# Summing gathered expert rows on TensorE in column strips, with up and down gathers alternating in sets of four

## The reference, cut to what matters

```python
u_sel = jnp.take(expert_down, ib, axis=0)
act = jnp.einsum('tkd,td->tk', u_sel.astype(jnp.float32), hb.astype(jnp.float32))
w = gb * jax.nn.gelu(act, approximate=False)
v_sel = jnp.take(expert_up, ib, axis=0)
return jnp.einsum('tk,tkd->td', w, v_sel.astype(jnp.float32))
```

## Time and profile before

| | |
|---|---|
| three timed runs | 4560.25, 4561.05, 4565.51 us (median 4561.05) |
| span of the profiled execution | 4559.0 us, 21846 instructions; no separate time of this execution is given |
| DVE busy | 3389.3 us, 74% |
| POOL busy | 2108.9 us, 46% |
| PE busy | 1629.2 us, 36% |
| queue of POOL's gathers | 147456 packets, 1073.81 MB, 57.7% of 16 engines' span |

### The profile page before, as it was taken

How to read it: one execution, slowest core, us unless ns; L and a number is a source line. 1 busy time by engine, 2 the same in 40 slices (tenths; PEclk the granted TensorE clock), 3 DMA queues, 4 the chain that set the end, 5 groups by cost and what they waited for, 6 DMA issues and landing times. The chain is left out here.

```text
span 4559.0 us, 21846 instructions
## 1 busy us (share of the span) xinstructions
PE 1629.2 (36%) x5521; PEld 961.5 (21%) x5521; DVE 3389.3 (74%) x4309; ACT 397.1 (9%) x780; POOL 2108.9 (46%) x1162
## 2 busy tenths in 40 slices
PE   8999978998900000000000099888000000000000
PEld 6444434444800000000000066457000000000000
DVE  3777795301099999999999913411999999999999
ACT  1111114300100000000000013301000000000000
POOL 0000000000076777776777700000777767767767
PEclk9999989999955555555555599799555555555555
DMA  6343422344399999999999953132999999999999
GB/s 201 111 110 112 117 67 85 103 142 144 126 411 397 379 398 400 378 396 394 388 394 400 374 159 132 56 129 76 405 387 394 400 382 394 408 384 390 398 389 377
DMA packets 283029, 1286.59 MB, mean 282 GB/s; under 512 B 46993, under 2 KB 56033, under 8 KB 150881
## 3 DMA queue, kind: packets, MB, share of 16 engines
q0 software_dynamic: 147456, 1073.81, 57.7%
q1 hardware_dynamic: 100400, 200.81, 13.6%
q10 hardware_dynamic: 35120, 11.33, 1.0%
HBM read 1283.77 MB, written 2.10 MB: 282 GB/s over the span
## 5 line engine op out<-in xcount | busy, mean ns | idle before, releaser
L1578 DVE SCALAR_TENSOR_TENSOR xs<-big,sc,xs 128x2048 f32<-128x2048 f32 x512 | 1203.7, 2351 | 51.0 <-DVE sc L1568 2.1
L1560 DVE CUSTOM_DVE_ANT_0 big<-big,hs 128x2048 f32<-128x2048 f32 x512 | 1137.8, 2286 | 34.8 <-remote 10.3
L488 POOL DMA_INDIRECT big<-in_peer_down,sc x256 | 518.2, 2024 | 638.0 <-issue 635.4
L531 PE MATMUL bank<-wring,ht 128*128 128x512 f32 (+1 forms) x1792 | 778.5, 592 | 3.3 <-ACT ht L888 1.7
L488 POOL DMA_INDIRECT big<-in_peer_u,sc x256 | 518.2, 2024 | 405.0 <-DVE sc L1547 320.4
L488 POOL DMA_INDIRECT big<-in_peer_up,sc x256 | 506.0, 1977 | 247.6 <-DVE xs L1578 172.2
L488 POOL DMA_INDIRECT big<-in_peer_v,sc x256 | 506.1, 1977 | 246.6 <-DVE xs L1578 171.1
L772 PE MATMUL bank<-cn,sc 80*128 80x80 f32 x1 | 0.4, 393 | 1381.4 <-DMA sc<-in_rec_out_norm_g 1381.4
L531 PEld LDWEIGHTS bank<-wring,ht 128*128 128x128 f32 x1792 | 339.7, 192 | 402.1 <-issue 395.9
L545 PE MATMUL bank<-ht,wring 128*128 128x256 f32 x1792 | 387.9, 379 | 2.6 <-ACT ht L888 2.6
L545 PEld LDWEIGHTS bank<-ht,wring 128*128 128x128 f32 x1792 | 340.2, 190 | 49.6 <-issue 2.4
(11 more groups left out here) (308 smaller groups left out, 2055.2 us busy)
## 6 DMA issues: line engine op xcount, KB each, us to landing
wring<-in_w_in SPq DMA_DIRECT2D x84, 1024.0 KB, 5.3
wring<-in_w_out SPq DMA_DIRECT2D x32, 1024.0 KB, 5.0
wring<-in_w_attn_o SPq DMA_DIRECT2D x16, 1024.0 KB, 5.1
wring<-in_peer_w_query SPq DMA_DIRECT2D x16, 1024.0 KB, 5.0
wring<-in_peer_w_q SPq DMA_DIRECT2D x16, 1024.0 KB, 5.0
wring<-in_glu_w_a SPq DMA_DIRECT2D x8, 1024.0 KB, 5.0
wring<-in_glu_w_b SPq DMA_DIRECT2D x8, 1024.0 KB, 5.0
big<-in_peer_down,sc POOLq DMA_INDIRECT x256, 9.5
```

The source lines that it names most:

```text
L488: pool.indirect_dma_start(out=gslot[:, slot, :], out_offset=None, in_=table[0], in_offset=bass.IndirectOffsetOnAxis(ap=usub(rST)[:, b * TO ...
L531: mm = pe.matmul(dense_bank[2 * pair + t][:, 0:w_cols], lhs[:, k, t * P:(t + 1) * P], wslot[:, b, kk * w_cols:(kk + 1) * w_cols], start=(k ...
L1560: v.tensor_tensor_reduce(gslot[:, slot, :], gslot[:, slot, :], h[:, t, :], 1.0, 0.0, ALU.mult, ALU.add, sub(rAC)[:, b * TOPK + kk:b * TOPK ...
L1578: v.scalar_tensor_tensor(x[:, t, :], gslot[:, slot, :], wt[:, kk:kk + 1], x[:, t, :], ALU.mult, ALU.add).then_inc(gused[slot], 1)
```

## The change

The dots stay on DVE as they are. The sum over the up rows moves to TensorE:

- An up gather still brings 128 rows of 8 KB, but now 16 experts of 8 tokens: partition 16 i + k holds expert k of token i of group g, and 16 such gathers (groups) make a unit. For this the expert numbers are needed "by row": DVE spreads them over 128 columns (`rIR`), TensorE multiplies with `tok_div` (`turn_indices`), and DVE copies the result to `rSTT` (`indices_by_row`). The weights take the same way (`turn_weights`), and DVE writes 16 blocks of 128x32 (`weight_blocks`), each with 8 filled columns.
- TensorE sums (`up_set`): a set is four gathers, groups s, 4+s, 8+s and 12+s, one for each strip q of 32 output partitions. For each of four banks of 512 columns it issues four matmuls, one per strip, and accumulates over the 8 heads of a tile in `acc_bank`. After a tile DVE adds the four banks to `x` (`add_experts`).
- The ring of 8 slots becomes 4 down slots and 4 up slots. POOL alternates: an up set of unit u-1, then a down set of unit u. A down gather waits for its own slot, an up set for the whole up set before it (`uused`). After the last down set the down slots serve every second up set.
- The loops over units are unrolled on POOL, ACT, DVE and TensorE.

The diff, cut to its core:

```diff
-GROUNDS = 2 * TOPK // SLOTS
+SETS = 4
+ROWS = TOPK // SETS
+TOK_G = P // TOPK
...
+            def fetch(slot, table, index, full):
+
+                pool.indirect_dma_start(
+                    out=slot, out_offset=None, in_=table[0],
+                    in_offset=bass.IndirectOffsetOnAxis(ap=index, axis=0)).then_inc(full, 16)
+
+            def gathers(layer, down, up):
+                base, n0 = layer * UNITS, layer * UNITS * SETS
+                pool.wait_ge(uused, n0)
+                for u in range(UNITS + 1):
+                    for s in range(SETS):
+                        if u:
+
+                            n, last = (u - 1) * SETS + s, u == UNITS
+                            if s == 0:
+                                pool.wait_ge(stage_t_ready, base + u)
+                            if last and s == 1:
+                                for k in range(SETS):
+                                    pool.wait_ge(dused[k], (layer + 1) * UNITS * ROWS)
+                            elif n:
+                                pool.wait_ge(uused, n0 + n - (last and s > 1))
+                            else:
+                                pool.wait_ge(sk_evac, 8 * (layer + 1))
+                            for q in range(SETS):
+                                g = q * SETS + s
+                                i = (u - 1) % 3 * TOPK + g
+                                slot = dslot[:, q, :] if last and s % 2 else uslot[:, q, :]
+                                fetch(slot, up, usub(rSTT)[:, i:i + 1], dfull[q] if last and s % 2 else ufull)
+                        if u < UNITS:
+                            if s == 0:
+                                pool.wait_ge(stage_ready, base + u + 1)
+                            for k in range(SETS):
+                                n = u * ROWS + s
+                                if n:
+                                    pool.wait_ge(dused[k], layer * UNITS * ROWS + n)
+                                i = u % 2 * TOPK + s * SETS + k
+                                fetch(dslot[:, k, :], down, usub(rST)[:, i:i + 1], dfull[k])
+
+            gathers(0, a["peer_down"], a["peer_up"])
...
+            def turn_indices(n):
+
+                pe.wait_ge(irep_ready, n + 1)
+                pe.matmul(vi_bank[:, 0:TOPK], sub(rIR), tok_div, start=True, stop=True).then_inc(vi_done, 1)
+
+            def turn_weights(n):
+
+                pe.wait_ge(wrep_ready, n + 1)
+                pe.matmul(v_bank[:, 0:TOPK], sub(rWR), tok_div, start=True, stop=True).then_inc(v_done, 1)
+
+            def up_set(layer, u, s):
+
+                if s == 0:
+                    pe.wait_ge(stat_ready, layer * UNITS + u + 1)
+                    if u % PH == 0 and (layer or u):
+                        pe.wait_ge(x_done, 4 * (layer * NT + u // PH))
+                from_d = u == UNITS - 1 and s % 2
+                if from_d:
+                    for q in range(SETS):
+                        pe.wait_ge(dfull[q], 16 * (layer * D_FILLS + UNITS * ROWS + (s + 1) // 2))
+                else:
+                    n = u * SETS + s - (u == UNITS - 1 and s == 2)
+                    pe.wait_ge(ufull, 64 * (layer * (UNITS * SETS - 2) + n + 1))
+                for c in range(4):
+                    for q in range(SETS):
+                        src = dslot if from_d else uslot
+                        mm = pe.matmul(acc_bank[c][32 * q:32 * q + 32, :], w_blocks[:, u % 2, q * SETS + s, :],
+                                       src[:, q, c * 512:(c + 1) * 512], start=(u % PH == 0 and s == 0),
+                                       stop=(u % PH == PH - 1 and s == SETS - 1), skip_group_check=True)
+                mm.then_inc(uused, 1)
+
+            def expert_sums(layer):
+                base = layer * UNITS
+                turn_indices(base)
+                for u in range(UNITS + 1):
+                    if u:
+                        turn_weights(base + u - 1)
+                        up_set(layer, u - 1, 0)
+                        up_set(layer, u - 1, 1)
+                    if u + 1 < UNITS:
+                        turn_indices(base + u + 1)
+                    if u:
+                        up_set(layer, u - 1, 2)
+                        up_set(layer, u - 1, 3)
...
-                act.wait_ge(gused[7], u * GROUNDS + 3)
+                act.wait_ge(acts_ready, u + 1)
...
-                v.scalar_tensor_tensor(usub(rST)[:, b * TOPK:(b + 1) * TOPK], sub(rIS)[:, 0:16], float(NKEY),
-                                       sub(rIS)[:, 16:32], ALU.mult, ALU.add).then_inc(stage_ready, 1)
+                st.link(v.scalar_tensor_tensor(sub(rIX), sub(rIS)[:, 0:16], float(NKEY), sub(rIS)[:, 16:32],
+                                               ALU.mult, ALU.add))
+                v.tensor_copy(usub(rST)[:, b * TOPK:(b + 1) * TOPK], sub(rIX)).then_inc(stage_ready, 1)
+
+                v.tensor_tensor(sub(rIR).rearrange("p (i k) -> p i k", i=TOK_G),
+                                sub(rIX).unsqueeze(1).broadcast_to([P, TOK_G, TOPK]),
+                                tok_mod.unsqueeze(2).broadcast_to([P, TOK_G, TOPK]),
+                                ALU.mult).then_inc(irep_ready, 1)
...
-            def unit_down(unit, b, t):
-
-                for kk in range(TOPK):
-                    slot = kk % SLOTS
-                    v.wait_ge(gfull[slot], (unit * GROUNDS + kk // SLOTS) * 16 + 16)
-                    v.tensor_tensor_reduce(gslot[:, slot, :], gslot[:, slot, :], h[:, t, :], 1.0, 0.0, ALU.mult,
-                                           ALU.add, sub(rAC)[:, b * TOPK + kk:b * TOPK + kk + 1]
-                                           ).then_inc(gused[slot], 1)
-
-            def unit_up(unit, b, t):
-
-                v.wait_ge(gelu_ready, unit + 1)
+            def indices_by_row(n, u):
+
+                if u >= 3:
+                    v.wait_ge(uused, (n - u + u - 2) * SETS)
+                v.wait_ge(vi_done, n + 1)
+                i = u % 3 * TOPK
+                v.tensor_copy(usub(rSTT)[:, i:i + TOPK], vi_bank[:, 0:TOPK]).then_inc(stage_t_ready, 1)
+
+            def down_set(layer, u, s):
+
+                t, b = u // PH, u % 2
+                for k in range(SETS):
+                    v.wait_ge(dfull[k], 16 * (layer * (UNITS * ROWS + 2) + u * ROWS + s + 1))
+                    i = b * TOPK + s * SETS + k
+                    v.tensor_tensor_reduce(dslot[:, k, :], dslot[:, k, :], h[:, t, :], 1.0, 0.0, ALU.mult, ALU.add,
+                                           sub(rAC)[:, i:i + 1]).then_inc(dused[k], 1)
+                if s == SETS - 1:
+                    v.wait_ge(dused[SETS - 1], (layer * UNITS + u) * ROWS + ROWS)
+                    v.sem_inc(acts_ready, 1)
+
+            def weight_blocks(n, u):
+
+                b = u % 2
+                v.wait_ge(gelu_ready, n + 1)
                 wt = sub(rWT)[:, b * TOPK:(b + 1) * TOPK]
                 st.link(v.tensor_tensor(wt, sub(rGT)[:, b * TOPK:(b + 1) * TOPK],
                                         sub(rGE)[:, b * TOPK:(b + 1) * TOPK], ALU.mult))
-                for kk in range(TOPK):
-                    slot = kk % SLOTS
-                    rnd = unit * GROUNDS + 2 + kk // SLOTS
-                    v.wait_ge(gfull[slot], rnd * 16 + 16)
-                    if kk:
-
-                        prev = (kk - 1) % SLOTS
-                        v.wait_ge(gused[prev], unit * GROUNDS + 2 + (kk - 1) // SLOTS + 2)
-                    v.scalar_tensor_tensor(x[:, t, :], gslot[:, slot, :], wt[:, kk:kk + 1], x[:, t, :], ALU.mult,
-                                           ALU.add).then_inc(gused[slot], 1)
-                v.wait_ge(gused[SLOTS - 1], unit * GROUNDS + 5)
-                v.sem_inc(turn_over, 1)
+                v.tensor_tensor(sub(rWR).rearrange("p (i k) -> p i k", i=TOK_G),
+                                wt.unsqueeze(1).broadcast_to([P, TOK_G, TOPK]),
+                                tok_mod.unsqueeze(2).broadcast_to([P, TOK_G, TOPK]),
+                                ALU.mult).then_inc(wrep_ready, 1)
+                if u >= 2:
+                    v.wait_ge(uused, (n - 1) * SETS)
+                v.wait_ge(v_done, n + 1)
+                v.tensor_tensor(
+                    w_blocks[:, b].rearrange("p (q r) c -> p q r c", q=SETS),
+                    v_bank[:, 0:TOPK].rearrange("p (q r) -> p q r", q=SETS).unsqueeze(3)
+                    .broadcast_to([P, SETS, SETS, 32]),
+                    col_mask.unsqueeze(1).broadcast_to([P, SETS, SETS, 32]), ALU.mult).then_inc(stat_ready, 1)
+
+            def add_experts(layer, t):
+
+                v.wait_ge(uused, (layer * UNITS + (t + 1) * PH) * SETS)
+                for c in range(4):
+                    xc = x[:, t, c * 512:(c + 1) * 512]
+                    v.tensor_tensor(xc, acc_bank[c][:, :], xc, ALU.add).then_inc(x_done, 1)
 
...
+                for u in range(UNITS + 1):
+                    if u:
+                        weight_blocks(base + u - 1, u - 1)
```

(66 more changed lines are left out.)

39 lines of the change are left out of this document (24 added, 15 removed).

## The result

The changed kernel takes **4704.07 us** (median of four runs, 4700.67 to 4718.27), the kernel before 4561.3: ratio 1.0317, 95% interval 1.0302 to 1.0333. The forecast was 5010. It is slower, as said, by 143 us where 449 were expected. The profiled execution took 4718.27 us, its span is 4716.4, so its times stand 14 us above the median.

What follows compares the result with a forecast made beforehand. DVE was taken to bound the kernel, DMA just behind. With P = 9.6 + 15.2 = 24.8, a layer of 76 + 1513 + 10 = 1599 us is 227 more, 454 for two: 5015, said as 5010 us; range 4400 to 5640.

Steps and rivals of the forecast that it cites:

- The bound and the floor: Expert stages: DVE bounds at 85.4 us per unit, DMA close behind; DMA needs at least 19.86 us per up-and-down pair.
- The loop and its formula: Expert stages: POOL issues the next up set only after TensorE finishes the last; a layer takes 76 + 61 P + E.
- P: Time from one up set's landing to the next: E + 15.2, forecast 24.8 us, or 19.86 if that is longer.
- E: Time TensorE takes to sum one up set of 16 matmuls (32 passes): forecast 9.6 us, bounds 7.3 to 14.5.
- E = 9.6: TensorE's set sum: 17 pass times, 4.6 us at half clock and the other 11.6 passes at full in 5.0.
- The restart of 15.2: From TensorE's set end to the next landing: 1.0 us for counts to be seen plus 14.2 for POOL's gathers.
- my 14.2: From POOL's issue to the fourth gather's landing on an empty DMA queue: 14.2 us, at least 12.9.
- The direction: Whole kernel: slower than before, by 227 us per layer and 454 for two; chance of slower 0.65.
- The rival with all four strips: TensorE's strips all run at once: E 5.7 us, kernel 4403 to 4531, faster if E is below 5.9; chance 0.31.
- Half clock through the stage: TensorE's clock stays at 1.2 GHz in the expert stages: E 14.5 us, P 29.7, kernel 5620; chance 0.20.
- strips without overlap: TensorE's 32 passes run one after another: E 16.1 us, P 31.3, kernel 5820, or 7200 at half clock; chance 0.13.
- What was priced at nothing: DVE's remaining 48 us per unit, `choose`, and the gelu-to-blocks chain of some 6 us: none bounds or adds time.

Runs made afterwards that it cites:

- the strips one after another: Changed kernel with a set's two loops swapped, all four banks of one strip before the next strip: 5178.31 us.
- half the columns: Changed kernel with two of the four banks summed, columns 1024 to 2047 left out: 4434.44 us, ratio 0.9716 to the kernel before.
- short dots: Changed kernel with every DVE dot taken over the first 256 of 2048 columns: 4515.69 us, ratio 0.9886 to the kernel before.
- full clock: Changed kernel with 18 unread matmuls (17 at small turns) filling TensorE's wait between up sets: 4480.55 us, ratio 0.9820 to the kernel before.
- half sets: Changed kernel with up slots in two halves, TensorE summing and freeing two strips at a time: 4436.59 us, ratio 0.9725 to the kernel before.
- the kernel with 15 fillers: Changed kernel with 15 unread matmuls after each set to keep TensorE's clock up: 4634.69 us, ratio 1.0136 to the kernel before.

## Why the prediction was wrong

- **The bound and the floor** held. DVE's additions were the bound, and DMA's floor of 19.86 us a pair is what the two best kernels reach: 20.1 and 2 x 10.0.
- **The loop and its formula** held. POOL waits for TensorE before each up set, and layer = 76 + 61 P + E gives 1442 of the measured 1445. With each run's measured E and P the tally follows the experiments too: for the strips one after another, 2 x (61 x 3.77 + 5.1) = 470 us over the change, measured 474; for half the columns 2 x (61 x 2.2 + 2.2) = 273 below, measured 270. That P itself follows E is what doubling, halving and reordering the matmuls show.
- **E = 9.6 is the step that failed.** I took 17 pass times from the reasoning that a matmul's second pass blocks the order; the trace has four passes at once and 8 pass times. The clock's part held: it rose after 4.4 us on average, and I had 4.6. Measured 5.8: 3.8 us too much in 62 places in each of two layers are 471 us.
- **The restart of 15.2** was 1.3 too small, 159 us. The count reached POOL sooner than I said: 0.5 on average where I had 1.0, of which 0.2 was counted twice, since my 14.2 ends with a dot that has already seen the landing. But from the first issue to the next set it took 16.1, not 14.2, and with short dots 14.7. So the dots make 1.4 of these 1.9 us; where the other 0.5 comes from stays open. Beside the dots the four issues took 1.75 us each, not the 0.94 of the earlier trace rows, which were issued with DVE idle. The long ones stood in my own rows, 2.39 beside an addition. The Trainium skill, "SBUF — State Buffer", SBUF: two separate sides, has the rule that would have warned me: a DVE instruction with two SBUF inputs locks the ports that it shares with GpSimd against a GpSimd operation that reads SBUF. The trace agrees as far as it goes, 0.94 us without a dot and 2.1 and more for the issues held beside one; that ports are the reason no run here shows. 5015 - 471 + 159 = 4703, against 4704. That it meets so closely is partly chance, since E and P are from an execution of 4718.
- **The direction was right by luck.** With the measured E of 5.8 and my restart of 15.2, my own sum gives 5015 - 471 = 4544 us, faster than before. Only the restart's 1.3 us, which I didn't price, make the change slower. Of the 449 us that I forecast 143 came.
- **The rival with all four strips** had E right (5.7) and the time wrong (4403 to 4531). It was to decide at E = 5.9; with a restart of 16.5 the point is (1296 - 61 x 16.5)/62 = 4.7. The change (5.8) lies above it and is slower; full clock (3.8) and half the columns (3.6) lie below and are faster; with short dots the restart is 15.2, the point 5.9, and 5.6 is faster. It also hoped that the queue would not empty. It does, in the pair shown for two microseconds. POOL issues some 6 us after the up set counts as landed, the first landing of a new issue takes 5.5, and of the 9.9 us of the down set up to 3 have gone by before TensorE starts, since DMA's engines are not in step.
- **Half clock through the stage and strips without overlap** did not come: in all 64 sets of the first layer the clock rose, within 6.0 us. What kept it at half in the 8.4 us of the earlier trace rows stays open.
- **What was priced at nothing** did cost nothing: DVE's 48 us a unit, `choose`, and the gelu chain lie beside a unit of 89 us. What was missed is that DVE's work still acts on POOL.
- On the rule of the Trainium skill, "TensorE: Matmul & The Clock Gate", Part 3, that matmuls start and end in strict order: this trace doesn't agree. Its loads come in fours, and four passes in a row for one strip don't hold up the other strips. The Trainium skill, "TensorEngine Tiling (Array Packing)", Theoretical Speedup, gives up to 4 times for 32 columns, and here the trace agrees: 32 passes in 8 pass times.

## What to carry to other kernels

When a ring's refill waits for the consumer of the whole ring, price the loop: consumer's time + restart from an empty queue, against the transfers that are still on their way meanwhile. Halving the grain of the hand-over (half sets, 268 us) was then worth as much as halving the consumer's work (270) and more than full clock for it (224), and TensorE still waited 4.5 us for its half (the line at 1727.59). Take an issue's length from a row in which the other engines do what they will do there, and where two rows disagree about a duration (0.94 and 2.39 here), ask what runs beside them before choosing one.

## What the runs showed of the hardware

- Passes of four 32-column strips start together, and a strip seems to take some four passes ahead; eight in a row for one strip leave at most two strips overlapping (E 10.9).
- TensorE's clock rose from half to full 2.6 to 6.0 us after a set of 32-column passes began (4.4 on average). In the kernel with 15 fillers a set after a wait of 1.6 us ran at full clock, one after 4.7 did not; between 2 and 4 us both happened.
- An indirect gather's issue takes 0.94 us on POOL. Held by a 128x2048 dot on DVE it takes up to 3.0 and ends 0.81 to 0.83 us after the dot; with dots of 256 columns the mean is 0.94.
- DMA's engines drift apart: of the 64 landing counts of an up set the last came 1.1 us after the 60th (median), in one pair 2.8, and the set starts with the last.
- Of four up gathers behind a drained queue the last is in, and the set starts, 14.6 us after the first issue when issues are short, and 16.0 when dots hold them up (medians of 60 pairs).
